# Modulation products of eight weight slots gathered in one PSUM bank before they are moved out

## The reference, cut to what matters

```python
def ada_params(cvec, w_ada, b_ada):
    return jnp.split(jax.nn.silu(cvec) @ w_ada + b_ada, N_ADA, axis=-1)
...
sa, ca, ga, sm, cm, gm = ada_params(c_lat, w_ada[l], b_ada[l])
sa_c, ca_c, ga_c, sm_c, cm_c, gm_c = ada_params(c_cx, w_ada[l], b_ada[l])
...
h = modulate(rms_norm(x, g_mix[l]), sa, ca)          # h * (1 + scale) + shift
```

## Time and profile before

| | |
|---|---|
| median of 3 runs | 3702.77 us (3702.67 to 3705.51) |
| the profiled execution, its own time | 3696.14 us |
| its span in the trace | 3694.8 us |
| granted TensorE clock, mean | 0.978 |
| PE busy | 94% of the span |
| POOL, DVE, ACT busy | 43%, 36%, 22% |
| L521, products of slots | 1536 records, 109.0 us |
| L533, turning into columns | 384 records, 59.2 us |
| L1170, copies of the rows | 96, 36.0 us |

### The profile page before, as it was taken

One profiled execution on the slowest core, in us unless ns is written; L12 is line 12 of the kernel. 1 busy time (PEld: TensorE's weight loads), 2 busy tenths in 40 slices (PEclk: granted clock), 3 DMA queues, 4 the chain that ended last, 5 costly groups with the idle time before them and its releaser, 6 DMA issues.

```text
span 3694.8 us, 43827 instructions
## 1 busy us (share of the span) xinstructions
PE 3491.5 (94%) x17956; PEld 2763.5 (75%) x17968; DVE 1332.5 (36%) x2278; ACT 821.8 (22%) x1689; POOL 1606.9 (43%) x1020
## 2 busy tenths in 40 slices
PE   5999999999999999999999699889999989979998
PEld 3667777788877677777778587778888877757886
DVE  5833322411157433123111555561211145652113
ACT  2234421100012334112010234420101113331111
POOL 2423255565654232664556331134333333235664
PEclk7999999999999999999999899999999999999999
DMA  6343223333333441234453210022433321113231
GB/s 203 103 127 113 86 77 106 103 92 98 88 95 108 145 134 36 91 103 134 129 160 86 83 49 24 23 71 92 140 99 115 108 63 49 35 57 126 91 99 61
DMA packets 409615, 351.07 MB, mean 95 GB/s; under 512 B 9797, under 2 KB 406853, under 8 KB 409418
## 3 DMA queue, kind: packets, MB, share of 16 engines
q1 hardware_dynamic: 401568, 340.82, 29.6%
q10 hardware_dynamic: 7850, 7.47, 0.7%
HBM read 346.16 MB, written 2.10 MB: 94 GB/s over the span
## 4 chain that ended last, share of the span: by engine, by line
PE 88%; DVE 6%; ACT 3%; issue 1%; DMA 1%; POOL 1%; ACTq 0%; DVEq 0%; POOLq 0%
PE psum L546 25%; PE psum L548 24%; PE psum L547 24%; PE psum L521 2%; PE psum L787 2%; PE psum L895 1%; PE psum L924 1%; DVE psum L1750 1%; PE psum L777 1%; PE psum L533 1%; PE psum L723 1%; PE psum L615 1%; DVE k L2230 1%; PE psum L764 1%; PE psum L766 1%
## 5 line engine op out<-in xcount | busy, mean ns | idle before, releaser
L496 POOL TENSOR_SCALAR weights_hi<-raw_weights 128x1024 fp32r<-128x1024 f32 (+3 forms) x508 | 508.3, 1001 | 2016.7 <-PE psum L548 1778.7
L546 PE MATMUL psum<-h_hi,weights_hi 128*128 128x512 f32 (+1 forms) x2896 | 1169.2, 404 | 64.7 <-DVE h_lo L1774 53.2
L499 POOL TENSOR_TENSOR weights_lo<-raw_weights,weights_hi 128x1024 fp32r<-128x1024 f32 (+3 forms) x508 | 1107.4, 2180 | 42.4
L547 PE MATMUL psum<-h_lo,weights_hi 128*128 128x512 f32 (+1 forms) x2896 | 1100.9, 380 | 0.0
L548 PE MATMUL psum<-h_hi,weights_lo 128*128 128x512 f32 (+1 forms) x2896 | 1100.9, 380 | 0.0
L546 PEld LDWEIGHTS psum<-h_hi,weights_hi 128*128 128x128 f32 x2896 | 550.2, 190 | 215.3 <-issue 99.4
L547 PEld LDWEIGHTS psum<-h_lo,weights_hi 128*128 128x128 f32 x2896 | 550.8, 190 | 118.0 <-issue 17.3
L548 PEld LDWEIGHTS psum<-h_hi,weights_lo 128*128 128x128 f32 x2896 | 549.5, 190 | 111.9
L546 PE MATMUL psum<-hidden_hi,weights_hi 128*128 128x512 f32 (+1 forms) x1120 | 411.9, 368 | 0.0
L547 PE MATMUL psum<-hidden_lo,weights_hi 128*128 128x512 f32 (+1 forms) x1120 | 411.6, 367 | 0.0
L548 PE MATMUL psum<-hidden_hi,weights_lo 128*128 128x512 f32 (+1 forms) x1120 | 411.2, 367 | 0.0
(11 more groups left out here) (261 smaller groups left out, 3731.9 us busy)
## 6 DMA issues: line engine op xcount, KB each, us to landing
raw_weights<-in_ada_w SPq DMA_DIRECT2D x96, 1024.0 KB, 5.3
raw_weights<-in_w_mlp SPq DMA_DIRECT2D x64, 1024.0 KB, 5.4
raw_weights<-in_w_in SPq DMA_DIRECT2D x56, 1024.0 KB, 5.2
raw_weights<-in_w_ffn_in SPq DMA_DIRECT2D x88, 512.0 KB, 5.2
raw_weights<-in_w_in SPq DMA_DIRECT2D x34, 512.0 KB, 4.6
raw_weights<-in_w_out SPq DMA_DIRECT2D x16, 1024.0 KB, 4.9
raw_weights<-in_w_ffn_out SPq DMA_DIRECT2D x16, 1024.0 KB, 5.0
raw_weights<-in_w_branch SPq DMA_DIRECT2D x56, 128.0 KB, 2.3
```

The costliest lines, as they stand in the source:

```text
L496: gpsimd.tensor_scalar(whi[:, r, c0:c1], raw[:, raw_slot, c0:c1], 1.0, 1.0, ALU.mult, ALU.mult).then_inc(*split_hi.up(*key, half))
L499: gpsimd.tensor_tensor(wlo[:, r, c0:c1], raw[:, raw_slot, c0:c1], whi[:, r, c0:c1].bitcast(F32), ALU.subtract).then_inc(*split.up(*key, half))
L546: tensor.matmul(out, sh, mh, start=first, stop=False, skip_group_check=shared)
L547: tensor.matmul(out, sh, ml, start=False, stop=False, skip_group_check=shared)
```

## The change

The slots of a group are taken in rounds of up to eight. `cond` gets 53 columns, with the three vectors in columns 21 to 23; slot c of a round uses a window of 32 columns that begins at 3 x (7 - c), so that its three rows fall on rows 3c to 3c + 2 of each strip, and zeros on the others. All slots of a round accumulate in one bank, which is moved out once by ACT and turned once by two matmuls with 24 moving columns. In a group of more than one round, PE turns a round after the first slot of the next one. A generator has n + 1 steps for n slots, and had n + 2. There are 18 rounds: one for each group, but two for feed and three for up2. `sel` has 24 columns per strip. DVE adds the bias round by round. For the larger `cond`, two bf16 constants move from the memory that lasts over the whole program to that of the first block, two inputs of the start move to its scratch memory, and the gates 4 and 5 of the column pairs behind the first go to the first 256 columns of `x`.

```diff
+def ada_rounds(group):
+
+    return [group[at:at + ROUND] for at in range(0, len(group), ROUND)]
+
-ADA_BANKS = {"start": ((0, 1), 2), "norm1": ((4, 5), 6), "norm2": ((4, 5), 6), "rope": ((6,), 7), "A": ((6,), 7),
-             "B": ((6,), 7), "feed": ((6,), 7), "gm": ((6,), 7), "up2": ((6,), 7)}
+ADA_BANKS = {"start": (0, 2), "norm1": (4, 6), "norm2": (4, 6), "rope": (6, 7), "A": (6, 7), "B": (6, 7), "feed": (6, 7),
+             "gm": (6, 7), "up2": (6, 7)}
+ROUND = 8
...
-    cond = top.take("cond", [P, KT, 32])
+    cond = top.take("cond", [P, KT, 32 + 3 * ROUND - 3])
...
-    gate = gat.take("gates", [P, 6, T])
+    gate = gat.take("gates", [P, 4, T])
...
     def gate_place(jj, g):
+        if jj and g < 4:
+            return gate[:, g, :].rearrange("p (a n) -> p a n", a=2)
         if jj:
-            return gate[:, g, :].rearrange("p (a n) -> p a n", a=2)
+            return X[:, 2 * g - 8:2 * g - 6, 0:TC]
...
         def ada_steps(name, l=None):        # tensor_engine
+            def columns(r):
+                layer, j = rounds[r][-1]
+                tensor.wait_ge(*ada_moved.at(layer, j))
+                if r == 0:
+                    tensor.wait_ge(*free[cols])
+                for h in range(2):
+                    at = 3 * ROUND * (2 * r + h)
+                    ins = tensor.matmul(bank[cols][:, at:at + 3 * ROUND], ada_rows[:, r % 2, h * P:h * P + P],
+                                        sel[:, 0:3 * ROUND], start=r == 0 and h == 0,
+                                        stop=r == len(rounds) - 1 and h == 1, skip_group_check=True)
...
+            for rnd, slots in enumerate(rounds):
+                for c, (layer, j) in enumerate(slots):
...
-                    tensor.wait_ge(*free[bk])
+                    if c == 0:
+                        tensor.wait_ge(*free[bk])
+                    at = 3 * (ROUND - 1 - c)
...
                     ins.then_inc(*ada_row.up("ada", layer, j))
...
+                    if c == 0 and rnd:
+                        columns(rnd - 1)
+                    yield
+                free[bk] = ada_moved.at(*slots[-1])
+            columns(len(rounds) - 1)
+            yield
...
         def ada_steps(name, l=None):        # scalar_engine
-            for c in range(n + 2):
-                if 1 <= c <= n:
...
-                    scalar.wait_ge(*ada_row.at("ada", layer, j))
-                    if c >= 3:
-                        scalar.wait_ge(*ada_col.at(*group[c - 3]))
-                    scalar.copy(ada_rows[:, q, :], bank[bk][:, 0:256]).then_inc(*ada_moved.up(layer, j))
-                yield
+            for r, slots in enumerate(ada_rounds(ADA[name if l is None else (name, l)])):
+                for _ in slots:
+                    yield
+                scalar.wait_ge(*ada_row.at("ada", *slots[-1]))
+                scalar.copy(ada_rows[:, r % 2, :], bank[bk][:, 0:256]).then_inc(*ada_moved.up(*slots[-1]))
...
+            yield
...
-    sel[32 * g, 0] = sel[32 * g + 1, 1] = sel[32 * g + 2, 2] = 1.0
+    sel[32 * g + np.arange(3 * ROUND), np.arange(3 * ROUND)] = 1.0
```

More of the change, by code:

```diff
@@ L335, in program @@
     one = Map(nc, top.at)
+    identb = one.take("identity_bf16", [P, P], BF16)
+    causal = one.take("causal_bf16", [P, P], BF16)
     hh = one.take("h_hi", [P, KT, T], F32R)
@@ L349, in program @@
     cm = tmp1.take("causal_f32", [P, P])
+    cond_in = tmp1.take("cond_in", [P, 3, KT])
+    cond_sigmoid = tmp1.take("cond_sigmoid", [P, 3, KT])
     pos = tmp1.take("pos_int", [P, T], I32)
@@ L508, in ada_steps @@
         def ada_steps(name, l=None):
-            group = ADA[name if l is None else (name, l)]
-            banks, cols = ADA_BANKS[name]
-            n = len(group)
-            for c in range(n + 2):
-                if c < n:
-                    bk, (layer, j) = banks[c % len(banks)], group[c]
+            rounds = ada_rounds(ADA[name if l is None else (name, l)])
+            bk, cols = ADA_BANKS[name]
+            def columns(r):
[8 more added lines that the diff above has]
+                                        stop=r == len(rounds) - 1 and h == 1, skip_group_check=True)
+                ins.then_inc(*ada_col.up(layer, j))
+                for slot in rounds[r]:
+                    ada_col.note(*slot)
+            for rnd, slots in enumerate(rounds):
+                for c, (layer, j) in enumerate(slots):
                     r = slab["ada", layer, j][0]
@@ L1709, in vector_engine @@
         for n in range(3):
[L1710 removed]
+            vector.tensor_tensor(cond[:, :, 3 * (ROUND - 1) + n], cond_in[:, n, :], cond_sigmoid[:, n, :],
                                  ALU.mult).then_inc(*dve_misc.up("cond"))
         def ada_finish(name, l=None):
[L1714 removed]
+            rounds = ada_rounds(ADA[name if l is None else (name, l)])
             cols = ADA_BANKS[name][1]
[L1716 to L1727 removed]
+            vector.wait_ge(*ada_col.at(*rounds[-1][-1]))
+            for r, slots in enumerate(rounds):
+                at, n = 0, len(slots)
+                found_columns = bank[cols][:, 6 * ROUND * r:6 * ROUND * r + 6 * ROUND].rearrange(
+                    "p (h c m) -> p c h m", h=2, m=3)
+                while at < n:
+                    (layer, j0), end = slots[at], at + 1
+                    while end < n and slots[end] == (layer, j0 + end - at):
+                        end += 1
+                    j1 = j0 + end - at
+                    for m in range(3):
+                        ins = vector.tensor_tensor(
+                            mod[:, 2 * j0:2 * j1, m].rearrange("p (c h) -> p c h", h=2), found_columns[:, at:end, :, m],
+                            ada_bias[:, layer, 2 * j0:2 * j1].rearrange("p (c h) -> p c h", h=2), ALU.add)
                     ins.then_inc(*mod_done.up(name, l))
[L1729 removed]
+                    at = end
         def norm_scales(g, sc, sh, m, key):
```

47 lines of the change are left out of this document (6 added, 41 removed).

## The result

The changed kernel takes 3660.39 us (median of 4 runs, 3658.79 to 3661.24), the kernel before, run beside it, 3704.14 us (4 runs, 3702.67 to 3705.62). The ratio is 0.9884, 95% interval 0.9871 to 0.9896, so 43.8 us less, where 49.7 were forecast. The profiled execution took 3658.79 us, span 3657.3, mean granted clock 0.978 as before. Between the two profiled executions only 37.4 us lie: the one of before was 6.6 us faster than the median of the runs in front, 8.0 faster than that of the runs shown here, and the one of after 1.6 faster than its own.

What follows compares the result with a forecast made beforehand. PE's matmul stream was taken as the bound. Pairs behind slots 24.9, pairs alone 2.2, attention waits 21.0, ninth step -2.4, rope 3.0 and start 1.0 sum to 49.7 us off 3702.8: 3653.1 us, range 3638 to 3674.

Steps and rivals of the forecast that it cites:

- A pair, 0.47 us: Behind a slot in attentions, feed, gm and up2: each removed pair of turning matmuls saves 0.47 us, 53 saving 24.9 us.
- the moved tensors, costed at nothing: Gates 4 and 5 in their new place: ACT writes either place in 0.69 us, so no cost was counted.
- attention B, 8.0 each: Attention B in each layer: without its waits for the bank and its pairs it should shrink by about 8.0 us.
- the first rival: Both attentions, as chains, take back their 30.6 us share: 3684 us if all, 3668 if half; chance 0.12.
- the emptied pipeline: In the attentions, each of 28 waits for the bank costs PE 0.17 us more than the idle shown.
- Attention A, 7.3 each: Attention A in each layer: without bank waits and pairs, less the new wait, it should shrink by about 7.3 us.
- The ninth step: In attention A, PE newly waits for the round's one copy: 1.03 us idle, 1.20 us in all, twice, so -2.4.
- Rope, 1.5 each: Rope: two waits gone (2.26 us), columns wait (-1.13), one pair gone (+0.36): 1.49 us per layer, 3.0 in all.
- The start, 1.0: At the start, ACT's one copy and the chain of squares begin earlier: 1.0 us taken, between 0 and 2.5.
- Free pairs: Rival: a pair's stationary loads run under the product before, so the 27.1 us do not come: 3680 us; chance 0.03.
- the third rival: More comes: attention A's map waits (3.5 us each), rope (2.07 per layer) and start: 62.3 us, time 3640; chance 0.10.
- the slower case: Rival: at round ends PE waits for ACT's copy; 4 us in each of 18 rounds gives 3725 us; chance 0.03.

Runs made afterwards that it cites:

- layout-only kernel: The kernel before with only the tensors moved as in the change (cond of 53 columns, constants, start inputs, gates); 3703.75 us, ratio 1.0007.

## Why the prediction was right, and where it missed

**Right in kind and nearly in size.** 3660.4 us lies in the range of 3638 to 3674, 7.3 us above the 3653.1. PE is still the bound, the stream of matmuls became shorter, and pairs and waits carry it: 14 to 15 and 24 to 27 us when put back one by one. The miss is larger where the forecast's own rows come from: for the profiled execution 3646.4 us was forecast and 3658.8 measured, and of the 49.7 us the traces show 37.5. That the medians miss by only 7.3 is in part luck: a usual execution of the kernel before is slower than the one whose rows were priced.

**A pair, 0.47 us.** Held nearly in feed, gm and up2: 4.5, 2.9 and 7.4 us against 4.6, 2.6 and 7.9, with 0.43 to 0.44 for a step of feed. A pair put back in front of a slot costs 0.34 us instead. That is a price of its place, or of its stationary operand that stays the same; this was not taken apart. So the experiment's 15.2 us for 63 pairs is not the forecast's 27.1 measured again.

**Failed: the moved tensors, costed at nothing.** The prediction priced the gates' new place by ACT's duration and found it equal; the other moved tensors got no price at all. The padding of 32 bytes in one experiment and the 96 or 224 in two others show that what counts is where the tensors *behind* the moved ones land. It cost 8 us in down2, the largest single line of the table, and gave some 4 to 5 back in the first block. Net it is some 3 us, less than attention B's 5.2 for both layers.

**Mis-sized: attention B, 8.0 each, measured 5.4.** Of the missing 2.6, 1.4 are the new wait for the map; it is the first rival in a small form, in the one stage where the prediction saw no sign of it, because the waits for the copy had covered it. Seven times the 0.10 us by which the emptied pipeline was priced too high make 0.7. The columns wait 0.9 us for their copy where they waited 0.6, 0.3 more. Together 2.4.

**Attention A, 7.3 each, measured 7.4 and 6.2.** The second layer is short by the same seven times 0.10 and by 0.5 us that the waits for the map grew (2.6 to 3.1). In the first layer these waits shrank instead, from 3.5 to 3.1. Before, it was 1.3 us longer than the other (81.3 against 80.0), 0.9 of that by one wait for the map (1.51 us against 0.59); they are equal to 0.04 now. The low clock at its entry is not shown to be the reason: the layout-only kernel has it too, with a wait of 0.54 and 80.3 against 80.2 us. The ninth step waits 0.94 us, forecast 1.03.

**Rope, 1.5 each, measured 1.7 and 0.7.** The mechanism was right to a few hundredths: the saved time turned into a wait of 2.32 us for POOL where some 2 were forecast, and the columns wait 1.04. What it does to the clock was not foreseen. The low stretch of some 3 us that follows the wait is new in the second layer, and costs about half its length; in the first it stands against the one before attention A that went.

**The start, 1.0, measured 0.3.** ACT's last copy starts 1.5 us earlier (40.12 against 41.66) and the load of the layer's columns 1.6 us earlier, but DVE loses it on the way to the squares: its scaling of `rope_sin` takes 1.95 us where it took 0.96, and the step on `norm_columns` behind it 0.88 where it took 0.17. The first squares on DVE start at 48.21 against 48.79. Why these two take longer is not shown.

**The rivals.** That the attentions take their share back happened to 1.4 us per layer in B and 0.5 in one A, not to 30.6. Free pairs were refuted. "3.5 us each" in the third rival was wrong from the start: the second layer's attention A waited 2.6 us for the map. No wait at the end of a round is longer than 1.04 us, so the slower case was far off. "More" did not come by itself; its term in rope did, once the slots stood one tile earlier.

## What to carry to other kernels

When a stream of matmuls is the bound, find the price of a small instruction from the distance of starts at its place, and look for the wait that hides under the wait you remove. A change that resizes or moves a tensor moves every tensor behind it: compare the pace of untouched inner loops before and after, in the trace, since a total can hide a gain and a loss. Print the byte offsets of the moving operands modulo 256 and try one padding for each; here that was worth about as much as the whole change. Look at every width of product: what made 512 columns faster made 256 slower.

## What the runs showed of the hardware

- Three matmuls of 512 moving columns with split float32 operands take 0.681 to 0.684 us when the moving operand lies at 128 modulo 256 bytes in a partition, and 0.697 to 0.703 at 0, 32, 64 and 96, with stationary operands at 128. That is 2 to 3% of the pace, at a granted clock of 1.00 in both cases.
- Three of 256 columns take 0.360 us (median) with the moving operand at 128 and 0.340 to 0.356 at 64 and 96; with moving weights at 128 they take 0.360 with the stationary operand at 128 and 0.351 to 0.353 at 64 and 96.
- Small float32 matmuls behind each other, with a stationary operand of 128 x 128 each, mostly start 0.11 us apart, with 3 moving columns as with 24. A pair of them, four records, costs 0.34 to 0.47 us by its place.
- After an idle PE of 2.1 to 2.3 us in rope the granted clock was 0.50 for some 3 us, in both layers of four traces. With the pairs back it stayed at 1.00 after 1.87 us in the first layer and fell after 1.80 us in the second. At the entry of attention A the same two waits (1.28 and 0.72 us) were followed by it in seven traces and not in seven, in the first layer. So a total can hold back what a removed wait should give: one edit that took four waits of 1 us away gave nothing by itself.
- A wait of PE ahead of a slot in the attentions costs 0.07 us beyond the idle time shown, at 14 of 14 slots.
- An untouched stage repeats to 0.1 us from trace to trace in most places (attention B in both layers: 97.7 to 97.9 before, again and with layout only; 92.35 to 92.38 in the changed kernel, again and in five variants that do not touch it), so that stages tell effects apart that the total, with its spread of 1 to 14 us, does not.
